# A two-layer encoder trunk on one core: the norms before the dense SwiGLU and the gMLP placed inside a projection of other tokens, attention's output projection in two passes, and the gMLP's u projection interleaved with its mixing

## The reference

```python
h = h + mixer_ab(rmsnorm(h, g1), w_in, rel_a, sinks, w_out, t5_bias)   # layer 0: two kinds of attention
h = h + dense_swiglu(rmsnorm(h, g2), wg, wu, wd)                       # (silu(x@wg) * (x@wu)) @ wd, 2816 wide
h = h + mixer_c(rmsnorm(h, g1), w_in, vg, ws, bs, w_out)               # layer 1: gMLP
h = h + moe_swiglu(rmsnorm(h, g2), wr, weg, weu, wed)                  # top 2 of 8 experts, 3584 wide
return rmsnorm(h, final_norm)

def rmsnorm(x, g):
    return x * rsqrt(mean(x * x, axis=-1) + 1e-6) * g

def mixer_c(h, w_in, v_norm_g, w_spatial, b_spatial, w_out):
    u, v = split(gelu(h @ w_in), 2)          # 1024 channels each
    v = rmsnorm(v, v_norm_g)                 # over the channels of a token
    # in blocks of 128 tokens and 8 groups of 128 channels: sv = mask(w_spatial[g]) @ v + b_spatial[g]
    return (u * sv) @ w_out
```

## Time and profile before

| | |
|---|---|
| time, median of 3 runs | 3848.09 us (3846.75 to 3864.86) |
| the profiled execution, its own time | 3827.89 us |
| its span, first to last instruction | 3826.1 us |
| mean granted clock of TensorE | 0.974 of 2.4 GHz |
| busy: PE / PE's weight loads / DVE / ACT / POOL | 94% / 91% / 45% / 43% / 3% |
| chain of work that ended last | PE 91%, DVE 4%, ACT 2%, issue 2%, DMA 1%, POOL 1% |
| stages by that chain | attention to 426 us; its output projection to 516; dense to 1278; gMLP to 1634; router to 1738; experts to 3765; end |

### The profile page before, as it was taken

The page is one execution under the profiler, slowest core; times in us unless marked ns, Lnnn a source line. Parts: engine busy times, 40 slices in busy tenths (PEclk is TensorE's granted clock), DMA queues, the critical chain, the costliest instruction groups (busy, mean ns, idle before and its releaser), DMA issues.

```text
span 3826.1 us, 77419 instructions
## 1 busy us (share of the span) xinstructions
PE 3599.4 (94%) x29808; PEld 3484.0 (91%) x29808; DVE 1724.0 (45%) x2452; ACT 1644.5 (43%) x2290; POOL 99.8 (3%) x132
## 2 busy tenths in 40 slices
PE   8999899998999889968999999999999999999993
PEld 6888789998999789938999999999999999999993
DVE  4455433323332433244555555555554444444444
ACT  3445323323332322135556465564654544544542
POOL 1000000000000000020000000000000000000001
PEclk9999999999999999989999999999999999999997
DMA  5111313232333311155665656656655445454446
GB/s 175 34 54 43 116 52 97 93 99 74 97 94 99 105 50 33 50 121 187 197 205 195 207 194 197 200 191 208 192 194 177 161 160 187 165 170 166 153 160 233
DMA packets 150303, 534.18 MB, mean 140 GB/s; under 512 B 17976, under 2 KB 18016, under 8 KB 149936
## 3 DMA queue, kind: packets, MB, share of 16 engines
q1 hardware_dynamic: 126288, 459.86, 36.9%
q0 software_dynamic: 14624, 55.52, 4.0%
q10 hardware_dynamic: 9280, 17.24, 1.5%
HBM read 502.93 MB, written 33.28 MB: 140 GB/s over the span
## 4 chain that ended last, share of the span: by engine, by line
PE 91%; DVE 4%; ACT 2%; issue 2%; DMA 1%; POOL 1%; ACTq 0%; POOLq 0%; DVEq 0%
PE ps L288 85%; PE ps L337 1%; PE ps L529 1%; PE ps L514 1%; PE ps L468 1%; PE ps L1293 0%; PE ps L1322 0%; DMA y<-yrow_d,slot 0%; PE ps L549 0%; PE ps L537 0%; PE ps L1087 0%; DVE rstd L319 0%; POOL tok_d L1269 0%; DMA tok_d<-tokid,slot 0%; PE ps L492 0%
## 5 line engine op out<-in xcount | busy, mean ns | idle before, releaser
L275 DVE TENSOR_TENSOR wl<-wraw,wh 128x1024 fp32r<-128x1024 f32 x860 | 1052.3, 1224 | 1542.3 <-ACT wh L271 1542.2
L271 ACT ACTIVATE wh<-wraw 128x1024 fp32r<-128x1024 f32 x860 | 904.0, 1058 | 1178.3 <-PE ps L288 1168.9
L288 PE MATMUL ps<-exh,wh 128*128 128x240 f32 (+3 forms) x3584 | 1018.5, 284 | 11.7 <-issue 9.5
L288 PE MATMUL ps<-exl,wh 128*128 128x240 f32 (+3 forms) x3584 | 1017.7, 284 | 0.0
L288 PE MATMUL ps<-exh,wl 128*128 128x240 f32 (+3 forms) x3584 | 1017.6, 284 | 0.0
L288 PEld LDWEIGHTS ps<-exh,wh 128*128 128x128 f32 x3584 | 676.5, 189 | 12.7 <-issue 12.7
L288 PEld LDWEIGHTS ps<-exl,wh 128*128 128x128 f32 x3584 | 676.4, 189 | 0.0
L288 PEld LDWEIGHTS ps<-exh,wl 128*128 128x128 f32 x3584 | 676.4, 189 | 0.0
L288 PE MATMUL ps<-mah,wh 128*128 (+4 forms) x1792 | 509.3, 284 | 0.6
L288 PE MATMUL ps<-mah,wl 128*128 (+4 forms) x1792 | 508.2, 284 | 0.0
L288 PE MATMUL ps<-mal,wh 128*128 (+4 forms) x1792 | 507.6, 283 | 0.0
(11 more groups left out here) (282 smaller groups left out, 4322.9 us busy)
## 6 DMA issues: line engine op xcount, KB each, us to landing
wraw<-in_w_expert SPq DMA_DIRECT2D x676, 512.0 KB, 3.9
wraw<-in_w_main SPq DMA_DIRECT2D x184, 512.0 KB, 3.6
yrow_d<-yst ACTq DMA_DIRECT2D x16, 512.0 KB
yT<-in_xT POOLq DMA_DIRECT2D x4, 1024.0 KB, 10.9
hT<-in_xT POOLq DMA_DIRECT2D x1, 4096.0 KB, 14.7
h_d<-hT POOLq DMA_DIRECT2D x1, 4096.0 KB, 14.8
hT<-h_d POOLq DMA_DIRECT2D x1, 4096.0 KB, 12.4
xrow_d<-rows ACTq DMA_DIRECT2D x16, 256.0 KB
```

What stands on the lines that cost most here:

```text
L271: act.activation(wh[:, j], wraw[:, j], ACT.Copy).then_inc(hi_done, 1)
L275: dve.tensor_tensor(wl[:, j], wraw[:, j], wh[:, j].bitcast(F32), ALU.subtract).then_inc(lo_done, 1)
L288: mm = pe.matmul(out[:, s], a, b[:, s], start=first and part == 0 and c == 0, stop=last and part == 2 and c + w == n)
```

## The change

No arithmetic of the model changes beyond the order of sums. The parts:

1. **Activations by half.** `xh` and `xl` become `xs[:, half, part, k]`, so that one token half can be rewritten while the other is read. `xdh` and `xdl` go; the dense part reads `xs[:, 0]`.
2. **Output projection of attention in two passes**, all eight units for tokens 0 to 511, then all eight again for 512 to 1023. SP loads the eight units twice. hT comes in two DMAs of one half each.
3. **Four norms (m = 0 to 3) beside other work.** Their squares are added up over the chunks by DVE (`acc_dve`, 7 adds of 128 x 512), so that PE needs one matmul against ones a norm (`sum_pe`). Norm 0 (dense, half 0) runs in the second pass of the output projection; norm 1 (dense, half 1) in the down projection of half 0; norm 2 (gMLP, half 0) in that of half 1; norm 3 (gMLP, half 1) in the v projection of half 0. The norms at the start and before the router stay as they were.
4. **The PSUM banks of dense half 1** are swapped with those of half 0, so that its first units do not wait for the adds.
5. **v projection by token half** (g), then by channel half (c); the eight units of `w_in` for v are loaded once for each g, 16 loads in place of 8. `product` issues it, and the v projection of attention, with 512 columns a matmul (`wide=True`). The v norm of tokens 0 to 511 runs beside the v projection of the others.
6. **u and mixing interleaved**, unrolled: PE runs u(u, half 0), mixing of group u - 1, u(u, half 1). z is split by halves as it comes; POOL reloads hT once `vgl` of the last group is made.

```diff
-        def product(pe, out, a_hi, a_lo, b_hi, b_lo, first, last):
+        def product(pe, out, a_hi, a_lo, b_hi, b_lo, first, last, wide=False):
             n = b_hi.shape[-1]
-            w = COLS if n == 2 * COLS else n
+            w = COLS if n == 2 * COLS and not wide else n
...
+        BESIDE = ((1, 0, 0), (1, 1, 0), (2, 0, 0), (2, 1, 1))
+        def square_act(act, m, k):
+            g, src, dst = BESIDE[m]
+            if k >= 2:
+                act.wait_ge(d_acc, 8 * m + k - 1)
+            elif m >= 1:
+                act.wait_ge(d_lo, 8 * m)
+            act.activation(st[:, k % 2], hT[:, k, of_half(src)], ACT.Square).then_inc(d_sq, 1)
...
+        def sum_pe(pe, m, b):
+            pe.wait_ge(d_acc, 8 * m + 8)
+            pe.matmul(bank(b), ones[:], acc[:], start=True, stop=True).then_inc(d_sum, 1)
...
+        def out_proj_pe(pe):
             with pe.Fori(0, 2) as i:
-                proj_qk_pe(pe, i + q0, 0, 0, lambda half, k: pe.wait_ge(sp_lo, KD * n + k + 1), order)
-                for j in range(1, 4):
-                    proj_qk_pe(pe, i + q0, j, 2 * j)
-                pe.wait_ge(op_add, 8 * i + (16 * n + 8))
+                for j in range(4):
+                    pe.wait_ge(op_add, 4 * i + (j + 1))
+                    ready = (lambda k: pe.wait_ge(sp_lo, k + 1)) if j == 0 else None
+                    out_unit_pe(pe, i + QO, j, 0, j, ready, SPLIT_ORDER).then_inc(unit_used, 1)
+            pe.wait_ge(sp_lo, 10)
+            for u in range(KD):
+                if u >= 4:
+                    pe.wait_ge(op_add, A0 + 8 + u - 3)
+                out_unit_pe(pe, QO + 2 + u // 4, u % 4, 1, 4 + u % 4).then_inc(unit_used, 1)
+                if u == 0:
+                    sum_pe(pe, 0, 0)
...
         def dense_pe(pe):
             for half in range(2):
                 u0 = U_DENSE + half * PER_DENSE
-                norm_pe(pe, 2 + half)
-                gate_up_pe(pe, *at(u0), NF_D, HALF, (xdh, xdl), half * NF_D, 8 * (2 + half))
-                down_pe(pe, *at(u0 + 2 * NF_D), NF_D, HALF, ah, al, 4, (half + 1) * NF_D + 2)
-                down_pe(pe, *at(u0 + 2 * NF_D + NF_D // 2), NF_D, HALF, ah, al, 0)
-                pe.wait_ge(y_add, 8 * half + 8)
+                b = 4 * half
+                if half == 1:
+                    pe.wait_ge(y_add, 4)
+                gate_up_pe(pe, *at(u0), NF_D, HALF, x_half(0), half * NF_D, 8 * half, b)
+                if half == 0:
+                    pe.wait_ge(op_add, A0 + 2 * KD)
+                else:
+                    pe.wait_ge(y_add, 8)
+                down_pe(pe, *at(u0 + 2 * NF_D), NF_D, HALF, ah, al, 4 - b, (half + 1) * NF_D + 2,
+                        lambda: sum_pe(pe, half + 1, b))
+                pe.wait_ge(d_root, half + 2)
+                down_pe(pe, *at(u0 + 2 * NF_D + NF_D // 2), NF_D, HALF, ah, al, b)
...
         def mix_pe(pe):
-            norm_pe(pe, 4)
-            norm_pe(pe, 5)
+            pe.wait_ge(y_add, 12)
+            for g in range(2):
+                for c in range(2):
+                    if g == 1:
+                        pe.wait_ge(v_gelu, 4 * c + 4)
+                    elif c == 1:
+                        pe.wait_ge(d_root, 4)
...
+                        if g == 0 and c == 0 and j == 1:
+                            sum_pe(pe, 3, 4)
...
+            for u in range(NG):
+                part_u(u, 0)
+                if u >= 1:
+                    spatial(u - 1)
+                part_u(u, 1)
+            spatial(NG - 1)
+            mix_out_pe(pe)
```

More of the change, by code:

```diff
@@ L339, in xdst @@
         def xdst(half):
[L340 to L355, removed]
+            return lambda part, k: xs[:, half, part, k]
@@ L686, in attend_act @@
                     if t == 4:
-                        act.wait_ge(yd_in, 32)
+                        act.wait_ge(yd_in, 64)
                     for k in SPLIT[t]:
[L689 to L692, removed]
+                        y, hi, lo = turns_of(k)
+                        act.activation(hi, y, ACT.Copy).then_inc(sp_hi, 1)
+            for y, k, half in ENDS:
+                act.wait_ge((sA_y, sB_y)[k // 4], STEPS - 4 + 4 * half)
+                act.activation(xs[:, half, 0, k], y[:, of_half(half)], ACT.Copy).then_inc(sp_hi, 1)
         def least_a_dve(dve, u):
@@ new lines, in build, with out_unit_pe @@
+        A0 = 4
+        def out_unit_pe(pe, q, j, half, b, ready=None, order=tuple(range(KD))):
+            pe.wait_ge(lo_done, 4 * q + j + 1)
+            for i, k in enumerate(order):
+                if ready:
+                    ready(i)
+                mm = product(pe, bank(b), wtile(wh, j, k), wtile(wl, j, k), xs[:, half, 0, k], xs[:, half, 1, k],
+                             i == 0, i == KD - 1)
+            return mm
+        def out_proj_pe(pe):
+            with pe.Fori(0, 2) as i:
+                for j in range(4):
+                    pe.wait_ge(op_add, 4 * i + (j + 1))
[8 more added lines that the diff above has]
+                    sum_pe(pe, 0, 0)
@@ new lines, in build, with split_z_act, split_z_dve, mix_out_pe @@
+        Z_SP = 10
+        def split_z_act(act, k, half):
+            act.wait_ge(z_add, 4 * k + 2 * half + 2)
+            act.activation(xs[:, half, 0, k], yT[:, k, of_half(half)], ACT.Copy).then_inc(sp_hi, 1)
+        def split_z_dve(dve, k, half):
+            dve.wait_ge(sp_hi, Z_SP + 8 * half + k + 1)
+            dve.tensor_tensor(xs[:, half, 1, k], yT[:, k, of_half(half)], xs[:, half, 0, k].bitcast(F32),
+                              ALU.subtract).then_inc(sp_lo, 1)
+        def mix_out_pe(pe):
+            with pe.Fori(0, 2) as i:
+                for j in range(4):
+                    for half in range(2):
+                        pe.wait_ge(op_add, 8 * i + (A0 + 9 + 2 * j + half))
+                        ready = (lambda k, h=half: pe.wait_ge(sp_lo, Z_SP + 8 * h + k + 1)) if j == 0 else None
+                        out_unit_pe(pe, i + Q_OUT1, j, half, 2 * j + half, ready).then_inc((bank_full, unit_used)[half], 1)
@@ new lines, in spatial @@
+            def spatial(u):
+                b = 4 * (u % 2) + 2
+                pe.wait_ge(v_lo, u + 1)
+                if u >= 2:
+                    pe.wait_ge(z_add, 4 * (u - 2) + 4)
+                for t in range(NT):
+                    mm = product(pe, bank(b + t // 4, P, P * (t % 4)), vgh[:, t], vgl[:, t], wsh[:, u], wsl[:, u], True, True)
+                mm.then_inc(sv_mm, 1)
+            pe.wait_ge(ws_lo, 1)
+            for u in range(NG):
[3 more added lines that the diff above has]
+                part_u(u, 1)
@@ L1459, in _ @@
                 load_units(sp, src(2 * c), 0, c)
-            with sp.Fori(1, U_DENSE // 4) as i:
+            with sp.Fori(1, QO) as i:
                 for c in range(2):
                     load_units(sp, src(4 * i + 2 * c), i, c)
+            for half in range(2):
+                with sp.Fori(0, 2) as i:
+                    for c in range(2):
+                        load_units(sp, src(4 * i + (4 * QO + 2 * c)), i + (QO + 2 * half), c)
             for half in range(2):
```

534 lines of the change are left out of this document (343 added, 191 removed).

## The result

| | before | changed kernel |
|---|---|---|
| median of 4 runs | 3847.42 us (3844.32 to 3864.86) | 3814.19 us (3813.39 to 3816.36) |
| span of the profiled execution, clock | 3826.1 us, 0.974 | 3814.7 us, 0.983 |
| end of attention to router | 1207.6 us | 1153.4 us |
| busy: PE / weight loads / DVE / ACT | 94 / 91 / 45 / 43% | 96 / 92 / 46 / 44% |

What follows compares the result with a forecast made beforehand. PE was taken to bound the kernel. Attention's end to router would shrink by 112.9 us to 1094.7, attention's v projection by 1.9: 114.8 us off 3827.89 gives 3713.1, stated as a median of 3733 us, range 3706 to 3765.

Steps and rivals of the forecast that it cites:

- What bounds the kernel: Whole kernel: PE, busy 94% of the span; only less PE work or less time standing still or slow-clocked helps.
- the gaps close: First output projection to router: clock 1.00 in every stretch, no PE wait over 2 us, about 1095 us in all.
- Rival 3: Four moved norms: late hand-overs make PE wait and restart slowly, 7.5 us each, 30 in all; 3763 us, chance 0.16.
- The slack of 1 to 2 us: Dense start and v norm: moved DVE and ACT work covered by 1.8 and about 1.4 us.
- the first price: Attention's end to router: a 256-column matmul costs 0.1135 us in a stream; 718.9 us for dense, 261.4 for three projections.
- the pairs of the v projection at 0.2356 us: v projection: two narrow matmuls, 5.89 / 25 = 0.2356 us, taken as the upper bound for one wide matmul.
- The wide matmuls: gMLP's v projection: 384 matmuls of 512 columns taken at 0.2255 us each, 86.6 us.
- 1094.7 - 3.8 + 0.6: Attention's end to router: 1094.7 us was the region's forecast length, 3.8 us its four fp32 sums.
- What lies outside is nearly untouched: Outside attention's end to router: nearly no change, except 1.9 us saved in attention's v projection.
- the mark: Prediction wrong if attention's end to router takes over 1125 us or the experts' stretch changes by more than a few us.
- added 20 us in the end: Whole kernel: profiled execution was 20 us under the median, so the summed 3713.1 became 3733 us for the median.
- All four: Rivals: as summed, 3733 us (0.67); wide matmul streaming only, 3726 (0.13); late hand-overs, 3763 (0.16); wide matmul slow (0.04).
- The formula for a wider matmul: Wide matmuls: N / 2.4 + 2.5 ns, 215.8 ns at 512 columns; by it 576 would cost 5.6 us less than summed.

Runs made afterwards that it cites:

- e5: e4 with the four fp32 sum matmuls left out, each partition taking the root of its own sum of squares: 3745.99 us.
- e1: The changed kernel with only `vstat` (160 B a partition) put back in its old place: 3761.12 us, ratio 0.976 to the kernel before.
- e4: e1 with both v projections narrow again, two 256-column matmuls in place of one of 512: 3752.55 us, ratio 0.974.
- e9: The kernel before with 160 B of unused space in front of every tensor, moving weights and activations together: 3834.18 us, ratio 0.999.
- e12: The kernel before with 128 B more between weights and activations: 3871.79 us, ratio 1.008.
- e2: The kernel before with 160 B of unused space behind `tokl`, moving the activations but not the weights: 3927.31 us, ratio 1.019.

## Why the prediction was wrong

- **What bounds the kernel, and that the gaps close: right.** All four moved norms, the v norm and the hand-overs between groups stay covered; no stretch of the region has a wait of PE worth naming and the clock is 1.00 in all stretches but the first (0.97). Rival 3 (30 us for late hand-overs) did not happen. The slack of 1 to 2 us that I had counted at the tight places was enough.
- **The step that failed** is the first price: "One matmul of 256 columns costs 355.38 / 3132 = 0.1135 us in a stream". It was read correctly and carried over as if it belonged to the instruction. It belongs to the place of its operands, and even at one place it isn't fixed. The prediction's own rows had a second price for this instruction at the full clock: the pairs of the v projection at 0.2356 us, 0.1178 each. It took that for a property of the projection and did not ask what differed. With the distance that the moved `vstat` gives it is 0.1200: (6336 + 2304) x 0.0065 = 56 us of the 59 missing in the region. The wide matmuls start 0.2343 us apart in its timeline, 384 x 0.0088 = 3 us more than taken. e5 is the check of everything else in the sum: without the four sums and the wide form the steps give 1094.7 - 3.8 + 0.6 = 1091.5 us from the first output projection to the end of the gMLP, and the row above reads 1091.55. That profile caught an execution at the cheaper pace throughout, so it checks the counts and the overlap at that price; that it agrees to 0.1 us is luck.
- **"What lies outside is nearly untouched": wrong**, for the same reason. The prediction itself named the mark: the region over 1125 us, or the experts' stretch changed by more than a few us. Both came true.
- **The baseline.** I took prices from one execution, 20 us under its median, and added 20 us in the end. Now it can be said what kind of execution that was: in it both dense streams and all other streams but the v projection ran at 113.3 ns. The changed order, with its distance repaired, had the dear pace behind most of its sums; e1's region took 1128.8 us (426.3 to 1555.1), 34 more than the sum, of which 6048 x 4.3 ns = 26 are in the two dense rows. That is why e4 stands at 3752.6 and not at 3733.
- **No rival had it.** All four spoke of waits or of the wide form. The diff held the cause, as a line that moved an allocation. It adds no instruction, and the prediction never mentions it.
- **The formula for a wider matmul.** The Trainium skill, "TensorE: Matmul & The Clock Gate", section "Back-to-back issue gap", gives N / 2.4 + 2.5 ns for an isolated matmul: 215.8 for 512 columns, where the runs have 228.9 (e1) and 234.3 (the changed kernel), and 109.2 for 256, where they have 113.3 to 120.0. For a stream with a weight load before each matmul, which is what runs here, the same section gives about 81 ns at 128 columns and 131 at 512; the runs have 112 and 228.9 to 234.3. The prediction quoted the first as if it were for a stream. Neither holds in this kernel, and neither has a term for the distance.

## What to carry to other kernels

A price per matmul read from a trace holds only for the SBUF layout of that trace. When a change adds, drops or moves any tensor, even one of 32 bytes, compare the distance between weights and activations before and after (here its place modulo 256 B told the kernels apart), and when a whole kernel turns slower or faster in stretches that the change doesn't touch, pad that distance first; it costs one unused tensor to try. In a kernel bound by PE, look at counts in windows of equal length, since busy shares show 100% at either price.

## What the runs showed of the hardware

- The time of a 128 x 128 fp32r matmul of 256 columns in a full stream at clock 1.00 depends on the distance between the stationary and the moving operand in SBUF: 113.3 to 120.0 ns over the eight distances modulo 256 B. Moving both together changed nothing (e9, 0.999), and where the operands exchange roles the price is that of the opposite distance (v projection: 117.8 in the kernel before, 113.3 in e12). Over the whole kernel before the spread is 2% (e9 0.999, e2 1.019).
- At the distance of 192 B one stream of identical instructions has two locked paces, 113.3 and 117.8 ns (in 40 us 355 or 342). The pace held over thousands of matmuls and changed only at breaks. With the weights stationary, the profiles of 32, 64, 128 and 160 B have more than one price too, those of 0, 96 and 224 B only one. Kernels at distances 0, 32 and 96 vary by 2 to 8 us from run to run, those at 192 by 9 to 43.
- Halving the number of weight loads with 512 columns saved 1.6 us of 179.6: 228.9 ns for one wide matmul where two narrow ones took 235.6. At the narrow ones' cheaper pace they took 226.7 (e5).
- In the steady stretches of the expert items a matmul of 240 columns cost 111.7 to 113.3 ns in all profiles, and one of 128 columns in the mixing 112: so 128 columns were no cheaper than 240. With 288 columns it was 131.7 to 133.3 ns, with 304 columns 137.8 to 141.7.
